# Stacked high and low keys and values, third units in the output bank, and the scaling of the probabilities on ScalarE

## The chip, the cores and the metric

The kernel runs on one core of a Trainium2 chip, in one launch. The metric is the device time of that launch in microseconds (us), lower is better. Engines: PE is TensorE (matmuls and transposes), ACT is ScalarE, DVE is VectorE, POOL is GpSimd, SP is the queue that issues the weight loads.

## The reference

One decoder layer over 512 tokens of width 1024 in float32: a SwiGLU, a mixer, a cross-attention to 256 memory tokens, a second SwiGLU, each with a norm before and after. The mixer runs two head groups on one input projection. The part that the change touches is the "fox" attention, 8 heads of width 64, and the scaling of the probabilities in the memory attention (4 heads of width 256):

```python
s = einsum('bhqd,bhkd->bhqk', q, k) * Dh ** -0.5
s = s + c[t] - c[s]            # c: running sum of log forget gates, per head
s = where(k_pos <= q_pos, s, -inf)
p = softmax(s, axis=-1)
o = einsum('bhqk,bhkd->bhqd', p, v)
```

## The kernel before

Every float32 product is made of three faster ones: each operand is split into a rounded high part and the rest (low), and the kernel adds high x high, low x high and high x low in the accumulator. The helper `three` (L1424) issues these three matmuls. The high part is written by ACT (a copy that rounds), the low part by DVE (a subtraction). The weights go the same way: SP loads a block of 1024 columns, ACT rounds it (L634, w_hi), POOL subtracts (L578, w_lo); PE waits for both.

The fox attention is cut into 32 units: unit k is head k // 4 and query block i = k % 4, with 128 (i + 1) keys. The four engines each run a loop over steps k, written out by hand. In step k,

- PE: scores of unit k (mask product L1719, then the three products; at least 256 keys wide), `fill(k)`: one or two quarters (six matmuls of 512 columns each) of the three input projections that are still left, spread over the steps by the table FILL; if unit k - 3 ends a head, the product of its four probability blocks with the values (`output`, 12 matmuls into bank 3); then the transposes of unit k - 2 (L1731, one per 128 keys, into bank 2).
- ACT: the exponential of unit k with its sum (L841), the rounding of a weight block if one is due (`round_to`, in the steps 4, 7, 9, 12, 15, 18, 20, 23, 27, 30 and 32), the high part of the transposed probabilities of unit k - 2 (L851), and for a head that has ended the high part of its output (L832). In each step with i = 3 it first spreads the next head's running sum (L821).
- DVE: the maximum of unit k (L1155), reciprocal and scaling of unit k - 1 (L1128, L1130, `normalise`), the low part of the transposed unit k - 2 (L1168), the low part of an ended head's output (L1142); around steps 10 to 14 also the evacuation of a finished projection and three multiplications by decays (L1297).

Every queue is served in order. PE's transposes of unit k - 2 wait for its scaled probabilities (normed) and for the low part of unit k - 3 (pt_l), because both units use bank 2. A head's output waits for pt_l of its last unit and for the low part of the output before (y_l), because all heads use bank 3.

FILL gives one quarter to steps 1, 4, 5, 8, 9, 11, 12, 13, 16, 17, 20, 21, 23, 24, 25, 27, 28, 29, 33 and 34, none to step 0, and two to the others. Of the steps with i = 3, therefore, 11, 23 and 27 have one quarter.

Ahead of the attention ACT and DVE evacuate the projections of q, k and v (`in_evacuate`): per group of 128 columns DVE scales into tmp (L1272), ACT rounds (L792 for q, L795 for k, L799 for v), DVE subtracts (L1280, L1284, L1288). PE's first fill waits for the low values of the first two token blocks. Behind the attention the gated linear attention (`gla`) starts with a warm-up product (L1435) once bank 3 is read out, and then waits for ACT's two copies L906. The memory attention runs the same kind of loop over 16 units, with the scaling by the same helper `normalise`.

Of the kernel before, what the change touches and what calls it, by code (L numbers as in the profile page):

```python
# [35 lines left out]
P = 128  # L36
# [139 lines left out]
def build(nc, a, out):  # L176
    ctx = ExitStack()
    with ctx:
# [73 lines left out]
        k_hi_a = sb("k_hi_a", [P, 2, SEQ], F32R, at=shared + 102 * kib)  # L252
        k_hi_b = sb("k_hi_b", [P, 2, SEQ], F32R, at=shared + 60 * kib)
        k_lo = sb("k_lo", [P, 4, SEQ], F32R, at=shared + 72 * kib)
        v_hi = sb("v_hi", [P, TC, FOX_W], F32R, at=shared + 32 * kib)
        v_lo = sb("v_lo", [P, TC, FOX_W], F32R, at=shared + 40 * kib)
# [21 lines left out]
        fox_hi, fox_lo = (t[:, :, :].rearrange("p (c e) n -> p c e n", e=2)[:, :, 0, :] for t in (q_hi, q_lo))  # L278

# [70 lines left out]
        q_zero = sem("q_zero")  # L350
        q_even_hi = sem("q_even_hi")
# [16 lines left out]
        y_l = sem("y_l")  # L368

# [68 lines left out]
        def key_hi(c):  # L438
            return (k_hi_a, k_hi_b)[c // 2][:, c % 2, :]
# [9 lines left out]
        def s_bank(k):  # L449
            return bank[fox_slot(k) % 2]  # L450

# [115 lines left out]
        def _(gp):  # L567
# [45 lines left out]
            for n, t in enumerate((q_hi, q_lo)):  # L613
                for e in range(2):
                    heads = t[FOX_D * (1 - e):FOX_D * (2 - e), :, :].rearrange("p (c e) n -> p c e n", e=2)
                    gp.memset(heads[:, :, e, :].bitcast(F32), 0.0).then_inc(q_zero, 1)  # L616
                    gp.wait_ge(q_zero, 2 * n + e + 1)
# [10 lines left out]
        def _(act):  # L628
# [156 lines left out]
            def in_evacuate(g, ms=range(4)):  # L785
                b = bank[IN_BANK[g]:IN_BANK[g] + 4]
                for m in ms:
# [5 lines left out]
                    elif g == 1:  # L793
                        act.wait_ge(in_tmp, 4 + m + 1)
                        act.activation(key_hi(m), tmp[:, m, :], ACT.Copy).then_inc(in_hi, 1)  # L795
                    elif g in (2, 4):
                        wait_group(act, g, m)
                        act.wait_ge(hinv, 2)
                        act.activation((v_hi if g == 2 else gv)[:, m, :], b[m][:, :], ACT.Copy,  # L799
                                       scale=rinv_tok[:, m:m + 1]).then_inc(in_hi, 1)  # L800
# [21 lines left out]

            def fox_attention():

                def output(done):
# [5 lines left out]
                    r = slice(FOX_D * (hd % 2), FOX_D * (hd % 2 + 1))  # L831
                    act.activation(fox_hi[r, hd // 2, :], bank[3][r, :], ACT.Copy).then_inc(y_h, 1)  # L832

                for k in range(N_FOX + LATE + 2):
                    if k < N_FOX - 1 and k % TC == TC - 1:
                        cum_spread(k // TC + 1)
                    if k < N_FOX:
# [4 lines left out]
                                       bias=nmx[:, r], scale=-1.0, accum_out=rs[:, r]).then_inc(expd, 1)  # L842
                    if k <= N_FOX + LATE:
                        round_to(B_IN + KB * FILL_GROUPS[0] + 2 + sum(FILL[:k]) // 4)
                    if 0 <= k - LATE < N_FOX:
# [3 lines left out]
                        if hd:  # L849
                            act.wait_ge(pv_done, hd)  # L850
                        act.activation(pt_hi[:, 0:nk, i * P:(i + 1) * P],  # L851
                                       bank[2][:, 0:nk * P].rearrange("p (j n) -> p j n", n=P),
                                       ACT.Copy).then_inc(pt_h, 1)
                    output(k - LATE - 1)
                    if k == PAIR_TURN[1]:
# [4 lines left out]
            def mem_attention():  # L860
# [10 lines left out]
                for k in range(len(MEM_UNITS) + LATE + 1):  # L871
                    u = N_FOX + k
                    if k < len(MEM_UNITS):
# [4 lines left out]
                                       scale=rinv_tok[:, i:i + 1], accum_out=rs[:, r]).then_inc(expd, 1)  # L878
                    output(k - LATE - 1)
# [61 lines left out]
            def mixer():  # L941
# [8 lines left out]
                round_to(B_IN + KB * 2 + 3)  # L950
                in_evacuate(1, (0, 1))
# [62 lines left out]
        def _(dve):  # L1014
# [109 lines left out]
            def normalise(u, w):  # L1124
# [4 lines left out]
                dve.wait_ge(rsum, u + 1)  # L1129
                dve.tensor_scalar(prob[:, u % PROBS, 0:w], prob[:, u % PROBS, 0:w], rr[:, r], None,  # L1130
                                  ALU.mult).then_inc(normed, 1)

            def fox_attention():

                def output(done):
# [4 lines left out]
                    r, c = slice(FOX_D * (hd % 2), FOX_D * (hd % 2 + 1)), hd // 2  # L1140
# [942 lines left out]
```

## Time and profile before

| | us |
| --- | --- |
| median of 3 runs | 1178.94 (1178.93 to 1179.42) |
| the profiled execution, its own time | 1180.76 |
| the profile's span | 1179.0 |
| PE busy | 1157.9 (98%) |
| ACT busy | 451.6 (38%) |
| DVE busy | 356.2 (30%) |
| POOL busy | 490.1 (42%) |

The profile is of one execution. Its span is the time between the first and the last instruction on record; 1.8 us of the execution's time lie outside it. The granted clock of TensorE was 0.999 over the span. A matmul's duration on record overlaps its successor's, so what a matmul takes of PE's time is the distance between two starts. DVE, ACT and POOL serve one instruction after the other, and their durations can be added, less about 0.1 us of overlap for each on ACT.

### The profile page before, as it was taken

Reading aid. Unit: us, or ns where it says so; the run is one execution under the profiler, and the core shown is the slowest. Engines: PE = TensorE matmul, PEld = TensorE weight load, DVE = VectorE, ACT = ScalarE, POOL = GpSimd, SP = SyncE. Lnnn points to the kernel's source line nnn. Section 1 sums busy time; section 2 is a strip of 40 time slices with the busy share of each in tenths; the row PEclk is TensorE's granted clock in tenths of the full one; section 3 lists DMA queues with packets and bytes.
Section 4 is the critical chain, followed back from the end, with each engine's and each line's share of the span. In section 5 each row is a group of like instructions: output and inputs, shape, how many; then the busy total and the mean of one; then the engine's idle time right before and its main releaser. Section 6 shows DMA issues by size and latency. Waiting matters only on the chain.

```text
span 1179.0 us, 15227 instructions
## 1 busy us (share of the span) xinstructions
PE 1157.9 (98%) x5664; PEld 964.8 (82%) x5664; DVE 356.2 (30%) x718; ACT 451.6 (38%) x740; POOL 490.1 (42%) x223
## 2 busy tenths in 40 slices
PE   8999999999999999999999999999999999999998
PEld 7888888888888878787778988878888888888886
DVE  2131221220005274655554204744131131130003
ACT  6232232231215456455625534545433232232113
POOL 5444344344442633222314863425435435434441
PEclk9999999999999999999999999999999999999999
DMA  6232332322222222111213442213333333222232
GB/s 201 90 106 91 93 103 89 107 89 99 98 90 89 72 90 87 41 55 52 90 54 108 161 160 91 80 54 119 103 93 93 103 89 107 89 98 99 90 107 108
DMA packets 84989, 113.03 MB, mean 96 GB/s; under 512 B 8846, under 2 KB 53964, under 8 KB 84940
## 3 DMA queue, kind: packets, MB, share of 16 engines
q1 hardware_dynamic: 84848, 112.34, 29.5%
q8 instruction: 33, 0.54, 0.2%
q14 instruction: 16, 0.13, 0.0%
q10 hardware_dynamic: 92, 0.02, 0.0%
HBM read 110.24 MB, written 2.10 MB: 95 GB/s over the span
## 4 chain that ended last, share of the span: by engine, by line
PE 62%; issue 24%; POOL 10%; DVE 2%; DMA 1%; ACT 0%; POOLq 0%; SPq 0%; DVEq 0%; ACTq 0%
PE bank L1426 14%; PE bank L1430 13%; PE bank L1427 13%; POOL w_lo L578 10%; PE bank L1566 7%; PE bank L1572 6%; PE bank L1567 6%; PE bank L1467 1%; DVE h L1063 1%; DMA raw<-in_ffn_w_gu 1%; POOL q_hi L616 0%; POOL q_lo L616 0%; PE bank L1503 0%; DVE tmp L1052 0%; DMA raw<-in_mix_w_in 0%
## 5 line engine op out<-in xcount | busy, mean ns | idle before, releaser
L578 POOL TENSOR_TENSOR w_lo<-raw,w_hi 128x1024 fp32r<-128x1024 f32 x200 | 478.9, 2404 | 666.4 <-ACT w_hi L634 665.9
L1426 PE MATMUL bank<-xh,w_hi 128*128 128x512 f32 (+1 forms) x912 | 349.6, 383 | 0.1
L1427 PE MATMUL bank<-xh,w_lo 128*128 128x512 f32 (+1 forms) x912 | 348.3, 382 | 0.0
L1430 PE MATMUL bank<-xl,w_hi 128*128 128x512 f32 (+1 forms) x912 | 348.3, 382 | 0.0
L634 ACT ACTIVATE w_hi<-raw 128x1024 fp32r<-128x1024 f32 x200 | 209.0, 1057 | 350.8 <-DMA raw<-in_ffn_w_down 167.5
L1430 PEld LDWEIGHTS bank<-xl,w_hi 128*128 128x128 f32 x912 | 171.4, 188 | 33.6
L1426 PEld LDWEIGHTS bank<-xh,w_hi 128*128 128x128 f32 x912 | 171.5, 188 | 33.1 <-issue 0.8
L1427 PEld LDWEIGHTS bank<-xh,w_lo 128*128 128x128 f32 x912 | 171.5, 188 | 32.0
L1566 PE MATMUL bank<-w_hi,mid_hi 128*128 128x512 f32 x352 | 137.2, 390 | 0.0
L1567 PE MATMUL bank<-w_hi,mid_lo 128*128 128x512 f32 x352 | 137.0, 389 | 0.0
L1097 DVE TENSOR_TENSOR tmp<-bank,rinv 128x512 f32<-128x512 f32 x44 | 30.2, 685 | 343.7 <-PE bank L1430 327.7
L1572 PE MATMUL bank<-w_lo,mid_hi 128*128 128x512 f32 x352 | 130.5, 389 | 0.0
L743 ACT ACTIVATE tmp<-tmp 128x512 f32<-128x512 f32 x44 | 27.9, 633 | 152.3 <-DVE tmp L1097 152.3
L1566 PEld LDWEIGHTS bank<-w_hi,mid_hi 128*128 128x128 f32 x352 | 66.1, 188 | 14.1 <-DVE tmp L1098 0.6
L1567 PEld LDWEIGHTS bank<-w_hi,mid_lo 128*128 128x128 f32 x352 | 66.1, 188 | 13.7
L1572 PEld LDWEIGHTS bank<-w_lo,mid_hi 128*128 128x128 f32 x352 | 66.1, 188 | 13.7
L1052 DVE SCALAR_TENSOR_TENSOR bank<-bank,g_row 128x512 f32<-128x512 f32 x20 | 13.8, 690 | 129.7 <-ACT sq L681 129.7
L1566 PE MATMUL bank<-w_hi,xh 128*128 128x512 f32 x96 | 38.6, 402 | 2.0 <-POOL w_lo L578 1.1
L1052 DVE SCALAR_TENSOR_TENSOR tmp<-bank,g_row 128x512 f32<-128x512 f32 x12 | 8.2, 682 | 105.8 <-ACT sq L681 105.8
L1567 PE MATMUL bank<-w_hi,xl 128*128 128x512 f32 x96 | 37.5, 391 | 0.0
L1572 PE MATMUL bank<-w_lo,xh 128*128 128x512 f32 x96 | 36.3, 392 | 1.1 <-POOL w_lo L578 1.1
L1130 DVE TENSOR_SCALAR prob<-prob,rr 128x256 f32<-128x256 f32 (+3 forms) x48 | 35.0, 729 | 1.7
(238 smaller groups left out, 1283.8 us busy)
## 6 DMA issues: line engine op xcount, KB each, us to landing
raw<-in_ffn_w_gu SPq DMA_DIRECT2D x176, 256.0 KB, 2.9
raw<-in_ffn_w_down SPq DMA_DIRECT2D x88, 256.0 KB, 2.8
raw<-in_mix_w_in SPq DMA_DIRECT2D x48, 256.0 KB, 2.8
raw<-in_mem_w_kv SPq DMA_DIRECT2D x32, 256.0 KB, 3.1
raw<-in_mem_w_o SPq DMA_DIRECT2D x24, 256.0 KB, 2.9
raw<-in_mix_w_out SPq DMA_DIRECT2D x16, 256.0 KB, 3.0
raw<-in_mem_w_q SPq DMA_DIRECT2D x16, 256.0 KB, 2.8
h<-in_x SPq DMA_DIRECT2D x4, 512.0 KB, 6.3
```

The lines of the kernel that those rows point to most:

```text
L578: gp.tensor_tensor(w_lo[:, n % SLOTS, :], raw[:, n % SLOTS, :], w_hi[:, n % SLOTS, :].bitcast(F32), ALU.subtract).then_inc(lo_ready, 1)
L634: act.activation(w_hi[:, n % SLOTS, :], raw[:, n % SLOTS, :], ACT.Copy).then_inc(hi_ready, 1)
L743: act.activation(tmp[:, pair, :], tmp[:, pair, :], ACT.Silu).then_inc(silu_done, 1)
L1052: dve.scalar_tensor_tensor(out=weighted_at(n)[:, :], in0=out_bank(s, n)[:, :], scalar=POST_SCALE[s], in1=g_row[:, cols], op0=ALU.mult, op1 ...
L1097: dve.tensor_tensor(tmp[:, pair, :], b[pair][:, :], rinv[:, :], ALU.mult).then_inc(gate_scaled, 1)
L1130: dve.tensor_scalar(prob[:, u % PROBS, 0:w], prob[:, u % PROBS, 0:w], rr[:, r], None, ALU.mult).then_inc(normed, 1)
L1426: pe.matmul(dst, w[0], x[0], start=start, stop=False, skip_group_check=loose)
L1427: pe.matmul(dst, w[1], x[0], start=False, stop=False, skip_group_check=loose)
L1430: return pe.matmul(dst, w[0], x[1], start=False, stop=stop, skip_group_check=loose)
L1566: pe.matmul(dst, x[0][:, tok], w[0][:, cols], start=start, stop=False, skip_group_check=True)
L1567: pe.matmul(dst, x[1][:, tok], w[0][:, cols], start=False, stop=False, skip_group_check=True)
L1572: return pe.matmul(out_bank(s, m)[:, :], x[0][:, tok], w[1][:, cols], start=False, stop=end, skip_group_check=True)
```

## The change

Keys: each fox head gets a tile of its own (`key_hl`) with its high part in 64 of the 128 rows and its low part in the other 64. Queries: the high part is written to both halves of the rows (8 further copies on ACT, `query_twins`), the low part keeps zeros in the other half. Scores are then two products instead of three. Values: each head's 64 high and 64 low columns lie side by side (`v_hl`), so the product with the probabilities gives high rows and low rows in one pass, two products instead of three for each of the four blocks. The two halves of bank 3 then have to be added: ACT copies one half out (`fox_y`, y_part), DVE adds the other (y_sum, bank 3 is free again), ACT rounds (y_h, `round_rows`) and DVE subtracts (y_l, `low_rows`) one step later.

In the diff the first `normalise` is ACT's, the second DVE's.

Units with i = 2 are transposed into bank 3, which then waits for y_sum of the output before; units with i = 3 wait for the low part of unit i = 1 instead of that of their predecessor. The scaling of the probabilities (`normalise`) moves from DVE to ACT in both attentions, in step k for unit k - 1, between the exponential and the rounding of a weight block; DVE keeps the reciprocal (`inverse_sum`). POOL clears half as many tiles ahead of the attention.

```diff
+            def query_twins():
+                for hd in range(FOX_H):
+                    act.activation(q_hi[head_rows(hd + 1), hd, :], tmp[head_rows(hd), hd // 2, :],
+                                   ACT.Copy).then_inc(q_twin, 1)
...
-                        act.activation(key_hi(m), tmp[:, m, :], ACT.Copy).then_inc(in_hi, 1)
+                        for e, done in enumerate((k_even_hi, in_hi)):
+                            r = head_rows(e)
+                            act.activation(key_hl(2 * m + e)[r, :], tmp[r, m, :], ACT.Copy).then_inc(done, 1)
...
+            def normalise(u, w):
+                r = slice(u % 4, u % 4 + 1)
+                act.wait_ge(rsum, u + 1)
+                act.activation(prob[:, u % PROBS, 0:w], prob[:, u % PROBS, 0:w], ACT.Copy,
+                               scale=rr[:, r]).then_inc(normed, 1)
...
-                    act.activation(fox_hi[r, hd // 2, :], bank[3][r, :], ACT.Copy).then_inc(y_h, 1)
+                    r, other = fox_rows_of(hd), fox_rows_of(hd + 1)
+                    act.activation(fox_y[r, hd // 2, :], bank[3][other, :], ACT.Copy).then_inc(y_part, 1)
+                def round_rows(done):
...
+                    act.wait_ge(y_sum, hd + 1)
+                    act.activation(fox_hi[r, hd // 2, :], fox_y[r, hd // 2, :], ACT.Copy).then_inc(y_h, 1)
...
+                    if 0 < k <= N_FOX:
+                        normalise(k - 1, key_width(FOX_UNITS[k - 1][1]))
                     if k <= N_FOX + LATE:
                         round_to(B_IN + KB * FILL_GROUPS[0] + 2 + sum(FILL[:k]) // 4)
...
                     output(k - LATE - 1)
+                    round_rows(k - LATE - 2)
...
-            def normalise(u, w):
+            def inverse_sum(u):
                 dve.wait_ge(expd, u + 1)
                 dve.reciprocal(rr[:, r], rs[:, r]).then_inc(rsum, 1)
-                dve.wait_ge(rsum, u + 1)
-                dve.tensor_scalar(prob[:, u % PROBS, 0:w], prob[:, u % PROBS, 0:w], rr[:, r], None,
-                                  ALU.mult).then_inc(normed, 1)
...
+                    dve.wait_ge(y_part, hd + 1)
+                    dve.tensor_tensor(fox_y[r, c, :], bank[3][r, :], fox_y[r, c, :],
+                                      ALU.add).then_inc(y_sum, 1)
+                def low_rows(done):
...
                     dve.wait_ge(y_h, hd + 1)
-                    dve.tensor_tensor(fox_lo[r, c, :], bank[3][r, :], fox_hi[r, c, :].bitcast(F32),
+                    dve.tensor_tensor(fox_lo[r, c, :], fox_y[r, c, :], fox_hi[r, c, :].bitcast(F32),
                                       ALU.subtract).then_inc(y_l, 1)
...
-                    three(dst, (q_hi[:, hd, tok], q_lo[:, hd, tok]), (key_hi(c)[:, 0:w], k_lo[:, c, 0:w]),
-                          False, True, True).then_inc(scored, 1)
+                    pe.matmul(dst, q_hi[:, hd, tok], key_hl(hd)[:, 0:w], start=False, stop=False, skip_group_check=True)
+                    pe.matmul(dst, q_lo[:, hd, tok], key_hl(hd)[:, 0:w], start=False, stop=True,
+                              skip_group_check=True).then_inc(scored, 1)
...
-                    if k:
-                        pe.wait_ge(pt_l, k)
+                    hd, i = FOX_UNITS[k]
+                    if i == TC - 2:
+                        if hd:
+                            pe.wait_ge(y_sum, hd)
+                    elif k:
+                        pe.wait_ge(pt_l, k - 1 if i == TC - 1 else k)
...
-                        last = three(bank[3][:, q0:SEQ],
-                                     (v_hi[:, j, c * P:(c + 1) * P], v_lo[:, j, c * P:(c + 1) * P]),
-                                     (pt_hi[:, j, q0:SEQ], pt_lo[:, j, q0:SEQ]), j == 0, j == TC - 1, True)
+                        for pt in (pt_hi, pt_lo):
+                            last = pe.matmul(bank[3][:, q0:SEQ], v_hl[:, j, hd, :], pt[:, j, q0:SEQ],
+                                             start=j == 0 and pt is pt_hi, stop=j == TC - 1 and pt is pt_lo,
+                                             skip_group_check=True)
```

## Rows read from the trace of the kernel before

**Rows 1.** The page, part 1: busy us (share of the span) x instructions of each engine.
```profile
PE 1157.9 (98%) x5664; PEld 964.8 (82%) x5664; DVE 356.2 (30%) x718; ACT 451.6 (38%) x740; POOL 490.1 (42%) x223
```

**Rows 2.** Busy time by engine over the fox attention: us, PE, PEld, DVE, ACT, POOL, clock, DMA.
```profile
452.50:570.50 118.00, 114.19 (x602) 95.19 (x601) 67.09 (x183) 55.21 (x128) 28.71 (x12) 1.00 0.18 57
```

**Rows 3.** PE in order of time, the score products: start us, us, instruction.
```profile
452.77 0.28 PE L1427 MATMUL bank<-k_hi_a,q_lo 128*128 128x256 f32 x1
452.89 0.28 PE L1430 MATMUL bank<-k_lo,q_hi 128*128 128x256 f32 x1
...
458.97 0.39 PE L1427 MATMUL bank<-k_hi_a,q_lo 128*128 128x512 f32 x1
459.20 0.39 PE L1430 MATMUL bank<-k_lo,q_hi 128*128 128x512 f32 x1
```

**Rows 4.** PE, idle before the transposes L1731 of the attention (us, times).
```profile
  DVE pt_lo L1168: 2.5, 4
```

**Rows 5.** The start of the stage, ACT, DVE and PE in order of time [idle before].
```profile
451.57 0.75 DVE L1288 SCALAR_TENSOR_TENSOR v_lo<-bank,rinv_tok,v_hi 128x512 fp32r<-128x512 f32 x1 [7.79 <-ACT v_hi L799]
...
453.49 0.40 PE L1426 MATMUL bank<-xh,w_hi 128*128 128x512 f32 x1
```

**Rows 6.** Forms by line from 400 to 570 us: x | busy us, mean ns | idle before.
```profile
L1142 DVE TENSOR_TENSOR q_lo<-bank,q_hi 64x512 fp32r<-64x512 f32 x7 | 4.8, 688 | 1.7 <-ACT q_hi L832 1.7
...
L792 ACT ACTIVATE q_hi<-tmp 64x512 fp32r<-64x512 f32 x8 | 5.0, 630 | 1.4 <-DVE tmp L1272 1.2
...
L851 ACT ACTIVATE pt_hi<-bank 128x512 fp32r<-128x512 f32 x8 | 4.7, 585 | 1.4 <-PE bank L1731 1.4
...
L795 ACT ACTIVATE k_hi_b<-tmp 128x512 fp32r<-128x512 f32 x2 | 1.2, 624 | 0.0
```

**Rows 7.** ACT and PE in head 5, from the one transpose at 530.71.
```profile
530.71 0.27 PE L1731 MATMUL bank<-ident,prob 128*128 128x128 f32 x1
...
538.41 0.41 PE L1731 MATMUL bank<-ident,prob 128*128 128x128 f32 x2
...
533.28 0.72 ACT L841 ACTIVATE prob<-prob,nmx 128x512 f32<-128x512 f32 x1
...
533.99 1.06 ACT L634 ACTIVATE w_hi<-raw 128x1024 fp32r<-128x1024 f32 x1
534.94 0.38 ACT L851 ACTIVATE pt_hi<-bank 128x256 fp32r<-128x256 f32 x1
536.01 0.40 ACT L841 ACTIVATE prob<-prob,nmx 128x128 f32<-128x128 f32 x1 [0.69 <-DVE nmx L1155]
```

**Rows 8.** POOL and DVE in order of time, where both read SBUF.
```profile
433.88 2.40 POOL L578 TENSOR_TENSOR w_lo<-raw,w_hi 128x1024 fp32r<-128x1024 f32 x1 [3.48 <-ACT w_hi L634]
...
535.13 2.39 POOL L578 TENSOR_TENSOR w_lo<-raw,w_hi 128x1024 fp32r<-128x1024 f32 x1 [9.05 <-ACT w_hi L634]
548.74 2.38 POOL L578 TENSOR_TENSOR w_lo<-raw,w_hi 128x1024 fp32r<-128x1024 f32 x1 [11.23 <-ACT w_hi L634]
...
433.95 2.88 DVE L1238 TENSOR_TENSOR ls_min<-ls_min,ls_abs 128x512 f32<-128x512 f32 x1
...
535.35 0.42 DVE L1168 TENSOR_TENSOR pt_lo<-bank,pt_hi 128x256 fp32r<-128x256 f32 x1 [1.73 <-ACT pt_hi L851]
...
536.09 1.71 DVE L1130 TENSOR_SCALAR prob<-prob,rr 128x512 f32<-128x512 f32 x1
```

**Rows 9.** DVE and PE in head 2, which carries the decays.
```profile
495.36 2.64 DVE L1297 TENSOR_TENSOR gq<-tmp,gq 128x1024 f32<-128x1024 f32 x1
...
500.24 0.50 PE L1426 MATMUL bank<-pt_hi,v_hi 128*128 128x512 f32 x1 [0.62 <-DVE pt_lo L1168]
```

**Rows 10.** The end of the stage, ACT and PE.
```profile
571.14 1.08 ACT L906 ACTIVATE gla_a<-bank 128x512 f32<-128x512 f32 x2
...
571.90 1.13 PE L1435 MATMUL bank<-ones 128*128 128x512 f32 x2 [0.54 <-DVE q_lo L1142]
```

**Rows 11.** The page, part 5: the scaling of both attentions on DVE.
```profile
L1130 DVE TENSOR_SCALAR prob<-prob,rr 128x256 f32<-128x256 f32 (+3 forms) x48 | 35.0, 729 | 1.7
```

More of the change, by code:

```diff
@@ L251, in build @@
         q_lo = sb("q_lo", [P, FOX_H, SEQ], F32R, at=shared + 16 * kib)
[L252 to L256, printed above, removed]
+        k_hl_a = sb("k_hl_a", [P, 2, SEQ], F32R, at=shared + 102 * kib)
+        k_hl_b = sb("k_hl_b", [P, 4, SEQ], F32R, at=shared + 72 * kib)
+        k_hl_c = sb("k_hl_c", [P, 2, SEQ], F32R, at=shared + 60 * kib)
+        v_hl = sb("v_hl", [P, TC, FOX_H, P], F32R, at=shared + 32 * kib)
+        v_hi, v_lo = v_hl[:, :, :, 0:FOX_D], v_hl[:, :, :, FOX_D:P]
         gq = sb("gq", [P, 2, SEQ], at=shared + 48 * kib)
@@ L350, in build @@
         q_zero = sem("q_zero")
+        q_twin = sem("q_twin")
+        k_even_hi = sem("k_even_hi")
+        k_even_lo = sem("k_even_lo")
         q_even_hi = sem("q_even_hi")
@@ L368, in build @@
         y_l = sem("y_l")
+        y_part = sem("y_part")
+        y_sum = sem("y_sum")
         ke_turned = sem("ke_turned")
@@ L450, in s_bank, with fp_bank @@
             return bank[fox_slot(k) % 2]
+        def fp_bank(k):
+            return bank[3 if k % TC == TC - 2 else 2]
         def key_width(i):
@@ L612, in _ @@
             gp.wait_ge(lo_ready, B_IN + 6)
[L613 to L617, printed above, removed]
+            for e in range(2):
+                heads = q_lo[head_rows(e + 1), :, :].rearrange("p (c e) n -> p c e n", e=2)
+                gp.memset(heads[:, :, e, :].bitcast(F32), 0.0).then_inc(q_zero, 1)
+                gp.wait_ge(q_zero, e + 1)
             for n in range(B_IN + 6, -(-(B_IN + 6) // SLOTS) * SLOTS):
@@ L798, in in_evacuate @@
                         act.wait_ge(hinv, 2)
-                        act.activation((v_hi if g == 2 else gv)[:, m, :], b[m][:, :], ACT.Copy,
-                                       scale=rinv_tok[:, m:m + 1]).then_inc(in_hi, 1)
+                        dst, src = gv[:, m, :], b[m][:, :]
+                        if g == 2:
+                            dst, src = v_hi[:, m, :, :], src.rearrange("p (h d) -> p h d", d=FOX_D)
+                        act.activation(dst, src, ACT.Copy, scale=rinv_tok[:, m:m + 1]).then_inc(in_hi, 1)
                     elif g == 5:
@@ L1172, in fox_attention @@
                     output(k - LATE - 1)
+                    low_rows(k - LATE - 2)
                     for g in (3, 5):
@@ L1715, in scores @@
                     dst, tok = s_bank(k)[:, 0:w], slice(i * P, (i + 1) * P)
-                    c, part = hd // 2, slice(0, 2) if i else slice(1, 3)
+                    part = slice(0, 2) if i else slice(1, 3)
                     if hd == FOX_H // 2 and i == 0:
+                        pe.wait_ge(k_even_lo, 4)
                         pe.wait_ge(in_lo, 12)
@@ L1741, in output @@
                     if hd:
-                        pe.wait_ge(y_l, hd)
+                        pe.wait_ge(y_sum, hd)
                     else:
@@ L1904, in gla @@
                     last.then_inc(ke_turned, 1)
-                pe.wait_ge(y_l, Y_FOX)
+                pe.wait_ge(y_sum, Y_FOX)
                 warm_up(bank[2], 1)
```

60 lines of the change are left out of this document (43 added, 17 removed).

## The prediction

> **What bounds the kernel now.** I read the page first: PE is busy for 98% of the span [rows 1], so the time is PE's own instructions plus the few places where PE waits. Then the windows: the fox attention lasts 118.0 us, PE is busy in 114.2 of them, DVE in 67, ACT in 55 [rows 2]. Only here and in the memory attention does the change touch work, and the granted clock is 1.00, so all prices are at the full clock. Third, PE in order of time: two score products of 256 columns start 0.12 us apart, two of 512 columns 0.23 [rows 3]; 384 columns lie between, 0.17. Fourth, PE's waits: the transposes wait for pt_lo, the low part that DVE writes, 2.5 us in 4 places [rows 4]. Last, ACT, DVE and POOL around one such wait, for their order [rows 7, 8]. The reader is to see that PE has the work, but that ACT and DVE hand units to it through two in-order queues with little to spare in the steps with one quarter of fill.
>
> **The change, part by part.** *Products.* Each head loses four score products (256, 256, 384, 512 columns) and four value products (512, 384, 256, 256): 2 x (0.23 + 0.17 + 0.12 + 0.12) = 1.28 us a head, 10.2 us for eight. This is certain, and it is the whole gain on PE. Everything else is about what ACT and DVE do when PE comes sooner.
>
> *Ahead of the attention.* The eight query twins cost 8 x 0.63 [rows 6] = 5.0 us on ACT, right where DVE has its idle 7.8 us before v_lo and ACT waits for DVE to reach the keys: hidden; uncovered they would cost at most 5. But each pair of key copies becomes four of half the rows, and 64 rows cost what 128 do (630 against 624 ns [rows 6]): +1.3 us for heads 0 to 3, +1.3 for heads 4 to 7, both ahead of v_hi on ACT; of the first, some 0.8 hides in an idle wait of ACT. v_lo then starts 1.8 us later than 451.57, its two instructions (0.75 each) end at 454.9, and PE's first fill, before at 453.49, starts at about 455.0 [rows 5]: +1.6 with the second wait behind it. POOL's smaller clearing frees POOL when nothing waits for it: 0.
>
> *Scaling on ACT.* No row shows it; the nearest are ACT's copies, 0.38 us for 256 columns [rows 7] and 0.585 for 512 [rows 6]; below, 0.1 less each by overlap; above, the exponential of 512 columns with 0.72 [rows 7]. I take the copies, because it is one. It sits behind the exponential and in front of the rounding and pt_hi, so pt_hi comes 0.2 to 0.5 later in every step. DVE loses 32 scalings here, 729 ns on average [rows 11], most of it from blocking (below).
>
> *Bank 3 for the third unit.* The waits of [rows 4] go: the third unit no longer waits for the second's low part, nor the fourth for the third's. y_sum takes the place of y_l with equal instructions, so heads hand over bank 3 as before.
>
> *The head's output.* ACT has one more copy per head (0.59) and DVE one more subtraction (0.69 unblocked, as L1142 [rows 6]), both in the step with i = 3, in front of the next maximum. low_rows is new in kind: both inputs lie in SBUF, where L1142 had one in PSUM. POOL and such an instruction exclude each other here: L1238 came 0.07 us behind a POOL subtraction and took 2.88 us instead of about 0.7, ending 0.55 after POOL; the scaling at 536.09 took 1.71; pt_lo at 535.35, which reads PSUM, took 0.42 within the same POOL instruction [rows 8]. The Trainium skill says so too (SBUF — State Buffer, section "SBUF: two separate sides": whichever starts first holds the shared port pair for its whole instruction, also against a DVE instruction with two SBUF inputs); by it low_rows waits out POOL, by DVE's bare rate it would take 0.69, and the traces agree with the first; the whole comes to 1181.6 by the first and to rival A's 1175.0 by the second.
>
> *One head, worked out.* Zero is 530.71 [rows 7]. The block rounded in step 23 starts at 533.99 = 3.3, behind the exponential; now the scaling of 384 columns is first: 3.7. POOL starts 1.14 behind the rounding (535.13 - 533.99) and lasts 2.4: 4.8 to 7.2. pt_hi starts 0.95 behind the rounding, 4.65; y_h follows, 4.9 to 5.5; low_rows is ready at 5.6, inside POOL's time, and ends at 7.2 + 0.55 = 7.75. Behind it on DVE are the maximum of unit 24 (0.3), then on ACT its exponential, at 8.0 (before: 536.01 = 5.3), 0.4, and the scaling of unit 23, 0.6: 9.0. For that PE waits with the transposes of unit 23, before at 538.41 = 7.7: +1.3. Behind them until the next head PE saves 0.17 + 0.64, so the head takes 0.5 longer than before.
>
> *The sum over the heads.* A block is rounded in the same step as low_rows in steps 7, 15, 23 and 27; step 27 is like 23 (POOL at 548.74 [rows 8]): +0.5 each. Step 7 has two quarters, PE comes 1.36 later: the wait is 0.9, and 0.7 more before the value product, because step 9 rounds too: -1.3 + 1.6 = +0.3, with rests +0.6. Head 2: its value product waits for pt_lo at 500.24 already [rows 9]; ahead of that on the chain now stand the scaling of units 10, 11, 12 (0.4, 0.5, 0.2) and y_h with low_rows (0.8): +1.9, less the 0.64 of the shorter product: +1.2. The decay at 495.36 took 2.64 behind POOL and does so again. Head 3: a decay (1.2) now behind y_sum delays the maximum by 0.9, then low_rows as above: +1.3. Head 4 has no such collision: -1.3. The last head: -1.28 + 0.35 of wait: -0.9. The first: +1.6 - 1.3 = +0.3. Behind the attention ACT must do y_h before its two copies (1.08 [rows 10]); they end 3.1 us behind the last product, the warm-up (1.13) 2.6: +0.5. Memory attention: 16 scalings of 0.38 on ACT in steps of over 3 us: 0; uncovered, 0.3 each. Sum: 0.3 + 0.6 + 1.2 + 1.3 - 1.3 + 0.5 + 0.5 - 0.9 + 0.5 = +2.7 us. The profiled execution (span 1179.0, own time 1180.8) would come to 1183.5; the median of the runs is 1.8 lower, 1178.9 + 2.7 = 1181.6.
>
> **The rivals.** *A: low_rows isn't held, or not in front of PE (faster).* If POOL has not started when it comes, or it is the later one, low_rows ends at 6.3 instead of 7.75; each of the heads with steps 23 and 27 then gains 1.4, step 15 1.9, step 7 1.9: 6.6 less, 1175.0. For it: PE's queue may have slack I took too small, and [rows 8] has few cases. Against: ACT's order fixes POOL's start 0.8 us ahead of low_rows. *B: the work removed is the gain (faster still).* The new waits stay within those removed: 1178.9 - 10.2 = 1168.7, with the 2.5 of [rows 4] 1166. For it: PE is 98% busy. Against: the idle 3.8 us of the stage already stem from these queues. *C: the lateness reaches the value products (slower).* pt_lo of a head's last unit leaves PE only 0.3 us in the heads with a collision, by the same chain; if every link (waits between engines, scaling as dear as the exponential) takes 0.1 more, PE waits again there, 0.7 in each of five heads: 1185.1. *D: the twins or key copies reach the weights.* ACT's rounding for the last block ahead of the attention comes 1.3 late, and POOL then has 0.3 to spare: at most 1 us, within the range.
>
> **How the numbers follow.** 0.2% (2.4 us) is about what a measurement of this kernel can tell from no change. Forecast 0.44 (1178.5 to 1184 for itself), A 0.28, B 0.07, C 0.21. Slower by over 2.4 us begins at 1181.3: half of the forecast and nearly all of C, 0.42. Faster ends at 1176.6: B, most of A, 0.32. The rest 0.26. The range takes in A with its lower side and C: 1172 to 1186; below lies B with some of A, above a tail of C.
>
> **What would show it.** In the profile after: PE with 64 matmuls fewer (5600); PE's idle time in the stage up from 3.8 to some 16 us; the transposes L1731's successor waiting for the scaling on ACT in heads 1, 3, 5 and 6 by 1 to 3 us; low_rows at over 2 us four times out of eight, 0.7 otherwise; the first fill at 455. Wrong if low_rows is short throughout, if the waits of PE move to pt_lo, or if head 2 is no longer than before.

## The result and the profile after

| | before | after |
| --- | --- | --- |
| median of 5 runs, us | 1178.94 (1178.92 to 1179.42) | 1188.56 (1187.15 to 1192.11) |
| ratio | | 1.0085, 95% interval 1.0075 to 1.0096 |
| profiled execution, own time / span, us | 1180.76 / 1179.0 | 1192.11 / 1190.4 |
| granted clock over the span | 0.999 | 0.992 |

The change makes the kernel 9.6 us slower. The point forecast had the direction right (slower by 2.7), the size not: 1181.6 had been predicted, with 1186 as the upper end. The profiled execution is the longest of the five; the others ran at a clock of 0.994 to 0.996, and the shortest, 1187.15 us, had the highest. So the time after goes with the clock; in the kernel before it was 0.998 or more in all executions beside the experiments below.

The page of the changed kernel, part 1:

```profile
PE 1157.1 (97%) x5600; PEld 961.7 (81%) x5600; DVE 338.5 (28%) x682; ACT 484.2 (41%) x808; POOL 485.7 (41%) x221
```

PE has the 64 matmuls fewer that were foreseen, and yet 0.8 us less busy time only, against 10.2 expected [rows 1]. The windows of the changed kernel say why (us, then PE, PEld, DVE, ACT and POOL busy, the granted clock, DMA). The first is the whole fox attention, the others are parts of it:

```profile
452.10:581.00 128.90, 112.13 (x536) 91.34 (x535) 61.43 (x161) 75.59 (x170) 28.71 (x12) 0.93 0.16 50
480.00:500.00 20.00, 16.46 (x76) 12.89 (x76) 10.06 (x28) 11.04 (x25) 4.43 (x2) 0.91 0.14 45
500.00:520.00 20.00, 15.53 (x71) 12.44 (x70) 11.58 (x26) 9.76 (x24) 2.72 (x2) 0.91 0.17 52
520.00:540.00 20.00, 19.40 (x101) 16.07 (x100) 7.63 (x26) 15.29 (x34) 4.82 (x2) 1.00 0.17 54
540.00:560.00 20.00, 16.42 (x79) 13.23 (x77) 8.96 (x20) 10.80 (x24) 4.76 (x2) 0.91 0.09 29
560.00:575.00 15.00, 13.09 (x53) 11.06 (x54) 5.61 (x19) 8.01 (x19) 2.40 (x1) 0.77 0.14 45
```

Two things are new beside [rows 2]. PE is idle for 16.8 of 128.9 us instead of 3.8 of 118.0, as forecast ("up to some 16"). And the clock, which was 1.00 in the whole stage, is 0.93: this was in no step of the prediction. PE in order of time around the transposes of unit 23, in head 5, shows both:

```profile
545.83 0.66 PE L1801 MATMUL bank<-ident,prob 128*128 128x128 f32 x4 [2.47 <-ACT prob L855]
...
547.03 0.44 PE L1491 MATMUL bank<-xh,w_lo 128*128 128x512 f32 x1
547.26 0.63 PE L1494 MATMUL bank<-xl,w_hi 128*128 128x512 f32 x1
547.69 0.63 PE L1490 MATMUL bank<-xh,w_hi 128*128 128x512 f32 x1
548.12 0.63 PE L1491 MATMUL bank<-xh,w_lo 128*128 128x512 f32 x1
...
550.67 0.40 PE L1491 MATMUL bank<-xh,w_lo 128*128 128x512 f32 x1
550.90 0.40 PE L1494 MATMUL bank<-xl,w_hi 128*128 128x512 f32 x1
```

Products of 512 columns start 0.23 us apart up to 547.26 and again from 550.67, and 0.43 apart between: PE is at the lower of its two levels (1.2 instead of 2.4 GHz) for some 3.4 us, from 1.4 us after it has waited for the scaled probabilities. The same follows the waits that end at 516.6 (products 0.43 apart up to 519.6) and at 561.9 (from 563.7 to 567.5); there the four transposes right behind the wait are at the lower level already (1.11 us for the four, 0.66 in head 5). The waits of PE in the stage of the changed kernel (us in total, times, longest):

```profile
PE bank L1801 <- ACT prob L855: 9.0, 5, 3.0
PE bank L1490 <- DVE tmp L1332: 2.5, 2, 2.1
PE bank L1818 <- DVE pt_lo L1225: 2.1, 3, 1.3
PE bank L1490 <- DVE v_hl L1351: 1.8, 1, 1.8
PE bank L1490 <- POOL w_lo L597: 0.9, 1, 0.9
```

In the kernel before, PE waited in this stage for pt_lo, 2.5 us ahead of the transposes [rows 4] and 0.62 ahead of one value product [rows 9], and hardly for anything else. L1801 are the transposes, L855 is the scaling on ACT, L1818 are the value products. Now the chain ahead of unit 23, lines of ACT, POOL and DVE of the changed kernel in order of time, with some left out between; the one transpose that was taken as zero is at 536.28 here:

```profile
536.28 0.27 PE L1801 MATMUL bank<-ident,prob 128*128 128x128 f32 x1
...
539.15 0.73 ACT L885 ACTIVATE prob<-prob,nmx 128x512 f32<-128x512 f32 x1
539.85 0.62 ACT L855 ACTIVATE prob<-prob,rr 128x384 f32<-128x384 f32 x1
540.36 1.06 ACT L652 ACTIVATE w_hi<-raw 128x1024 fp32r<-128x1024 f32 x1
541.31 0.39 ACT L897 ACTIVATE pt_hi<-bank 128x256 fp32r<-128x256 f32 x1
541.50 2.39 POOL L597 TENSOR_TENSOR w_lo<-raw,w_hi 128x1024 fp32r<-128x1024 f32 x1 [7.62 <-ACT w_hi L652]
541.57 0.63 ACT L876 ACTIVATE q_hi<-q_flat 64x512 fp32r<-64x512 f32 x1
542.23 2.20 DVE L1199 TENSOR_TENSOR q_lo<-q_flat,q_hi 64x512 fp32r<-64x512 f32 x1
544.36 0.27 DVE L1212 CUSTOM_DVE_ANT_0 prob<-bank,cum_b 128x128 f32<-128x128 f32 x1
544.67 0.40 ACT L885 ACTIVATE prob<-prob,nmx 128x128 f32<-128x128 f32 x1 [2.48 <-DVE nmx L1212]
545.07 0.71 ACT L855 ACTIVATE prob<-prob,rr 128x512 f32<-128x512 f32 x1
```

L1199 is low_rows, L876 round_rows, L597 GpSimd's subtraction. Read from the bottom: PE waits for the scaling of unit 23, which is behind the exponential of unit 24, which waits 2.48 us for the maximum of unit 24, which is behind low_rows, and low_rows takes 2.20 us and ends 0.5 after POOL's subtraction. It has the links of the forecast, in their order; how long they are comes below.

### The profile page after: what moved, and what is told of

It is laid out like the page before. It is cut to its first block, busy times and chain, and to the rows that moved or that the text cites. A ratio compares the mean times of both kernels' runs of the same rounds, so it can differ in the third digit from the quotient of the medians.

```text
span 1190.4 us, 15133 instructions
## 1 busy us (share of the span) xinstructions
PE 1157.1 (97%) x5600; PEld 961.7 (81%) x5600; DVE 338.5 (28%) x682; ACT 484.2 (41%) x808; POOL 485.7 (41%) x221
## 4 chain that ended last, share of the span: by engine, by line
PE 61%; issue 26%; POOL 10%; DVE 2%; DMA 1%; ACT 0%; POOLq 0%; SPq 0%; DVEq 0%; ACTq 0%
PE bank L1490 13%; PE bank L1491 13%; PE bank L1494 13%; POOL w_lo L597 10%; PE bank L1630 6%; PE bank L1631 6%; PE bank L1636 6%; PE bank L1531 1%; DVE h L1113 1%; DMA raw<-in_ffn_w_gu 1%; POOL q_lo L634 0%; PE bank L1567 0%; DVE tmp L1102 0%; DMA raw<-in_mix_w_in 0%; DVE bank L1102 0%
## 5 line engine op out<-in xcount | busy, mean ns | idle before, releaser
L597 POOL TENSOR_TENSOR w_lo<-raw,w_hi 128x1024 fp32r<-128x1024 f32 x200 | 478.2, 2401 | 682.3 <-ACT w_hi L652 681.9
L1636 PEld LDWEIGHTS bank<-w_lo,mid_hi 128*128 128x128 f32 x352 | 66.1, 188 | 13.8
L1102 DVE SCALAR_TENSOR_TENSOR bank<-bank,g_row 128x512 f32<-128x512 f32 x20 | 13.8, 692 | 129.4 <-ACT sq L699 129.4
L885 ACT ACTIVATE prob<-prob,nmx 128x128 f32<-128x128 f32 (+3 forms) x32 | 18.0, 563 | 41.3 <-DVE nmx L1212 41.3
```

The costliest lines, as they stand in the source:

```text
L597: gp.tensor_tensor(w_lo[:, n % SLOTS, :], raw[:, n % SLOTS, :], w_hi[:, n % SLOTS, :].bitcast(F32), ALU.subtract).then_inc(lo_ready, 1)
L885: act.activation(prob[:, k % PROBS, 0:w], prob[:, k % PROBS, 0:w], ACT.Exp, bias=nmx[:, r], scale=-1.0, accum_out=rs[:, r]).then_inc(expd, 1)
L1102: dve.scalar_tensor_tensor(out=weighted_at(n)[:, :], in0=out_bank(s, n)[:, :], scalar=POST_SCALE[s], in1=g_row[:, cols], op0=ALU.mult, op1 ...
L1636: return pe.matmul(out_bank(s, m)[:, :], x[0][:, tok], w[1][:, cols], start=False, stop=end, skip_group_check=True)
```

## The experiments

Each was timed beside the kernel before, on the same chip; 5 to 8 on another chip than the rest. The kernel before ran at 1179.16 us beside 1 to 4, 1179.29 beside 5 to 8 and 1179.04 beside 9 to 12. Where medians of different groups are subtracted below, this 0.25 us is the least that they are uncertain by. The changed kernel was not timed again: whatever is subtracted from its 1188.56 us also carries its scatter, 1187.15 to 1192.11. Experiments 1 to 8 and 10 to 12 start from the changed kernel, 9 from the kernel before.

| # | kernel | us | ratio to before (95%) |
| --- | --- | --- | --- |
| 1 | scaling on DVE | 1180.14 | 1.0009 (0.9999 to 1.0019) |
| 2 | rows split three steps later | 1181.3 | 1.0019 (1.0009 to 1.0028) |
| 3 | both | 1174.72 | 0.9962 (0.9948 to 0.9976) |
| 4 | long waits of the transposes filled | 1185.77 | 1.0058 (1.0041 to 1.0075) |
| 5 | saved products put back | 1195.09 | 1.0135 (1.0118 to 1.0152) |
| 6 | third unit in bank 2 | 1195.14 | 1.0129 (1.0112 to 1.0146) |
| 7 | scaling on DVE, memory attention only | 1188.72 | 1.0082 (1.0065 to 1.0099) |
| 8 | 3 with the first values earlier | 1176.14 | 0.9967 (0.9957 to 0.9977) |
| 9 | before, with the fox scaling on ACT | 1183.22 | 1.0033 (1.0020 to 1.0045) |
| 10 | 3 with the saved products put back | 1181.91 | 1.0025 (1.0016 to 1.0035) |
| 11 | 3 with four scalings on ACT | 1173.46 | 0.9951 (0.9934 to 0.9967) |
| 12 | 4 with a fifth wait filled | 1186.18 | 1.0058 (1.0041 to 1.0075) |

**1. Scaling on DVE again, in both attentions.** ACT's two calls of `normalise` go, DVE's `inverse_sum` scales as well (only its new lines are shown):

```diff
 dve.reciprocal(rr[:, r], rs[:, r]).then_inc(rsum, 1)
+if scaled_width:
+    dve.wait_ge(rsum, u + 1)
+    dve.tensor_scalar(prob[:, u % PROBS, 0:scaled_width], prob[:, u % PROBS, 0:scaled_width], rr[:, r],
+                      None, ALU.mult).then_inc(normed, 1)
```

> The scaling of the probabilities goes back to DVE in both attentions; the stacked products, the units in bank 3 and the new path of the head's output stay. Theory L (low_rows, blocked behind POOL in steps 7, 15, 23 and 27, makes the long waits of PE; the scaling only lengthens ACT's queue by about 0.4 us a step): low_rows still lasts about 2.1 us four times, the waits before the transposes of units 15, 23 and 27 fall from 3.4, 2.9 and 3.4 us to about 2, and with them the stretches at the clock's lower level: 1179 to 1183. Theory S (the scaling on ACT, 0.70 us for 512 columns where a copy takes 0.585, is itself the loss): the waits shrink below 1 us, and the time falls below 1175.

1180.14 us (1178.07 to 1181.88), inside theory L's range: 8.4 of the 9.6 us are gone. low_rows is as long as in the change, four times over 2 us (first row, duration in ns: shortest, median, longest), and the transposes still wait, but three times and at most 2.0 us (second row). The profiled execution is the fastest of the ten, with a clock of 0.999; the ten fall apart by the clock: three at 1178.1 us with 0.999, seven at 1180.1 to 1181.9 with 0.995 or 0.996. So in this kernel too the clock is lowered more often than not, and those executions are 2 us or more longer. low_rows by its line, and one of the waits:

```profile
L1199 DVE TENSOR_TENSOR q_lo<-q_flat,q_hi x8: 685/1378/2209, 476.0 to 569.8; 64x512 fp32r<-64x512 f32 x8
```

```profile
PE bank L1801 <- DVE prob L1177: 5.4, 3, 2.0
```

**2. The rows split later.** ACT's round_rows and DVE's low_rows move from the step with i = 3 to the next one with i = 2, ahead of pt_hi and pt_lo there; the scaling stays on ACT. The same edit in both queues:

```diff
+if k <= N_FOX + LATE:
+    low_rows(k - LATE - TC - 1)
 if 0 <= k - LATE < N_FOX:
     ...
 output(k - LATE - 1)
-low_rows(k - LATE - 2)
+if k == N_FOX + LATE + 1:
+    low_rows(k - LATE - 2)
```

> Scaling on ACT as in the change, but the rounding and subtraction of a head's output (round_rows, low_rows) are moved by three steps, into the long step with i = 2 ahead of the transposed probabilities, where both engines wait for PE anyway. Theory L: low_rows no longer stands in front of the maximum of the next head's first unit, the waits of PE before units 15, 23 and 27 fall to under 1.2 us, the clock stays at its upper level, 1173 to 1178. Theory S: the waits stay over 2 us, above 1184.

1181.3 us, 7.3 us less than the change, but between the two theories and in neither range. The waits of the transposes for the scaling fell as theory L had it, to 1.0 at most and 3.4 us in all instead of 9.0; the time did not, since PE now waits for pt_lo. In their new place the rows are held by POOL twice of eight times (2.46 and 2.34 us, else 0.69), and pt_lo is late for it by 0.5 and 0.8 us (third row: L1807 are the transposes, L1824 the value products). The longest wait, 2.9 in head 2, has no row in front of it: it is behind a decay (L1367) that took 2.68 us, and kernel 4 below has the same one. DVE of this kernel in order of time, and its waits:

```profile
518.91 2.46 DVE L1202 TENSOR_TENSOR q_lo<-q_flat,q_hi 64x512 fp32r<-64x512 f32 x1 [2.57 <-ACT q_hi L876]
521.30 0.27 DVE L1230 TENSOR_TENSOR pt_lo<-bank,pt_hi 128x128 fp32r<-128x128 f32 x1
```

```profile
PE bank L1824 <- DVE pt_lo L1230: 4.6, 3, 2.9
PE bank L1807 <- ACT prob L855: 3.4, 6, 1.0
PE bank L1807 <- DVE pt_lo L1230: 1.4, 2, 0.8
```

**3. Both edits.**

> Both edits of the two runs before this one together: scaling on DVE, and the head's output rounded three steps later. If L and S are separate links of one chain, this is the fastest of the three, 1169 to 1173, with some 4 us of idle PE in the stage. If either alone is the loss, it equals the better of the two within 1 us.

1174.72 us (1174.14 to 1174.87), faster than both kernels and the fastest of the three, though 1.7 us above the range. The two edits bring 8.4 and 7.3 us by themselves and 13.8 together, so they are two links and not one; some 1.9 us of what each brings is the same.

**4. The long waits filled.** The changed kernel with 1, 10, 8 and 10 idle products of 512 columns ahead of the transposes of units 7, 15, 23 and 27, into the bank that these then overwrite:

```diff
-pe.wait_ge(normed, k + 1)
 hd, i = FOX_UNITS[k]
 ...
+for _ in range({7: 1, 15: 10, 23: 8, 27: 10}.get(k, 0)):
+    pe.matmul(fp_bank(k)[:, :], ident_r[:, :], xh[:, 0, :], start=True, stop=True, skip_group_check=True)
+pe.wait_ge(normed, k + 1)
```

> The change itself, and in PE's queue ahead of the wait for the scaled probabilities 1, 10, 8 and 10 products of 512 columns into bank 2 (units 7, 15, 23 and 27), whose results the transposes then overwrite: they fill waits and add no result. Theory C (a wait of 2.4 us or more is followed by some microseconds at 1.2 GHz, which cost time by themselves): matmuls after those three waits start 0.23 us apart instead of 0.43, and the time falls by 3 to 5 us, to 1184 or 1185. If the clock costs nothing because PE would wait again anyway: 1188 to 1189.

1185.77 us (1185.59 to 1186.16; the shortest of the change is 1187.15), theory C at a little less than its price: PE does 6.6 us more of useless work, and the kernel is 2.8 us faster. The windows over heads 5 and 6 have a clock of 1.00 where the change had 0.91 and 0.77:

```profile
540.00:560.00 20.00, 18.65 (x96) 15.33 (x95) 10.17 (x26) 10.83 (x27) 3.93 (x2) 1.00 0.16 53
560.00:575.00 15.00, 14.50 (x75) 11.88 (x74) 6.42 (x16) 8.30 (x17) 4.81 (x2) 1.00 0.16 52
```

**5. The saved products put back.** A third score product and a third value product, as repeats of products that are there; the output differs from the reference for it.

```diff
+pe.matmul(dst, q_lo[:, hd, tok], key_hl(hd)[:, 0:w], start=False, stop=False, skip_group_check=True)
 pe.matmul(dst, q_lo[:, hd, tok], key_hl(hd)[:, 0:w], start=False, stop=True,
           skip_group_check=True).then_inc(scored, 1)
...
-for pt in (pt_hi, pt_lo):
+for n, pt in enumerate((pt_hi, pt_lo, pt_lo)):
```

> The changed kernel with TensorE's saved work put back: a third product into every score unit and a third value product for every token block, 1.28 us a head or 10.2 us in all at the full clock; the repeated products stand in for the removed ones and change the output. Theory 1, the chain of ScalarE, VectorE and GpSimd sets the pace at the waits: much of the added work only fills waits, the clock stays at 1.00 for longer, and the time rises by 2 to 6 us, to 1190 to 1194. Theory 2, TensorE's work sets the pace: the whole 10 us is added, 1198.

1195.09 us, 6.5 more, just above the range of theory 1. Of the 10.2 us of products some 6.5 show even in a kernel that waits this much. The reading is that the steps behind a wait are PE's own and only what lies ahead of one is free; which products were free was not traced.

**6. The third unit back in bank 2**, with the old wait for the low part of the unit before:

```diff
-return bank[3 if k % TC == TC - 2 else 2]
+return bank[2]
...
-if i == TC - 2:
-    if hd:
-        pe.wait_ge(y_sum, hd)
-elif k:
-    pe.wait_ge(pt_l, k - 1 if i == TC - 1 else k)
+if k:
+    pe.wait_ge(pt_l, k)
```

> The changed kernel with the third unit of every head back in bank 2, as before, waiting for the low halves of the unit before; all else as changed. Theory 1, the place of the third unit only moves a score product and its wait by a few tenths of a microsecond, and what releases the turns is further down the chain: 1188 to 1190. Theory 2, the early third unit crowds ScalarE and VectorE in the last steps of a head and is part of the loss: 1184 to 1186. Theory 3, the early start is what the change has in its favour, and without it each head waits longer: 1192 or more.

1195.14 us, 6.6 more: theory 3. In its waits the low parts are back, and longer than [rows 4] had them, since pt_hi is later:

```profile
PE bank L1798 <- DVE pt_lo L1225: 17.4, 11, 2.5
```

**7. Scaling on DVE in the memory attention alone.**

```diff
-if 0 < k <= len(MEM_UNITS):
-    normalise(u - 1, NMEM)
...
-inverse_sum(u - 1)
+inverse_sum(u - 1, NMEM)
```

> The changed kernel with the probabilities of the memory attention alone scaled by VectorE again, as before; those of the forgetting attention stay on ScalarE. Theory 1, the memory attention keeps TensorE busy either way, so that the whole loss lies in the forgetting attention: 1188, within 0.7 us. Theory 2, a part of the 8.4 us that came back with both scalings on VectorE lay here: 1184 to 1186.

1188.72 us (1187.45 to 1190.69), nothing that can be told from the change: theory 1. From 740 to 800 us PE is busy for 56.50 us here and 56.81 in the change.

**8. Kernel 3 with the values of two token blocks ahead of the second pair of key copies on ACT** (DVE's waits for these copies are numbered anew):

```diff
-in_evacuate(1, (2, 3))
 in_evacuate(2, (0, 1))
+in_evacuate(1, (2, 3))
```

> Scaling on VectorE in both attentions and the split of the output rows three steps later, as in the version that ran at 1174.72, and besides it the high values of the first two token blocks ahead of the second pair of key copies on ScalarE. Theory 1, the first fill's wait of 2.04 us at 451.85 goes, since it waits for the low values, and with it the time falls by 1 to 2 us: 1173 to 1174. Theory 2, the key copies that are now later are wanted just as soon, and the wait moves there: 1174.7 or a little more.

1176.14 (1174.20 to 1176.38) against 1174.72 (1174.14 to 1174.87): no gain. The wait only moves, as theory 2 had it, though to the other values and not to the keys. The first fill starts at 451.85 without waiting; the second waits 2.00 us for the other two token blocks, whose v_lo starts at 454.31, since ACT has the key copies and a weight block ahead of them. PE and DVE of this kernel in order of time:

```profile
451.85 0.40 PE L1496 MATMUL bank<-xh,w_hi 128*128 128x512 f32 x1
...
454.31 1.41 DVE L1357 SCALAR_TENSOR_TENSOR v_hl<-bank,rinv_tok,v_hl 128x512 fp32r<-128x512 f32 x2 [2.32 <-ACT v_hl L822]
...
455.87 0.47 PE L1496 MATMUL bank<-xh,w_hi 128*128 128x512 f32 x1 [2.00 <-DVE v_hl L1357]
```

**9. The kernel before with one part of the change alone**: ACT scales the fox probabilities, behind the exponential of the next unit.

```diff
+if 0 < k <= N_FOX:
+    r, w = slice((k - 1) % 4, (k - 1) % 4 + 1), key_width(FOX_UNITS[k - 1][1])
+    act.wait_ge(rsum, k)
+    act.activation(prob[:, (k - 1) % PROBS, 0:w], prob[:, (k - 1) % PROBS, 0:w], ACT.Copy,
+                   scale=rr[:, r]).then_inc(normed, 1)
```

> The kernel before with one part of the change alone: ScalarE scales the probabilities of the forgetting attention, right after the exponential of the next unit. Products, banks, values and output rows are as before, and no row is split from SBUF. Theory 1, the scaling on ScalarE is dear wherever TensorE waits for it (0.38 to 0.70 us a unit, and behind the next exponential): 1183 to 1188. Theory 2, it is dear only together with the longer way of the output rows that the stacked values bring; alone it even goes past the scalings that GpSimd's subtraction holds on VectorE: 1178 to 1180.

1183.22 us, 4.2 more. It is dear by itself (theory 1), at the lower end. Ahead of the transposes PE waits for pt_lo 7 times instead of 4 [rows 4], for more than twice the time:

```profile
PE bank L1737 <- DVE pt_lo L1174: 5.9, 7, 1.6
```

**10. Kernel 3 with the saved products put back**, by the edit of experiment 5; the output differs.

> The version that ran at 1174.72 (scaling on VectorE, output rows split three steps later) with TensorE's saved products put back as repeats, 1.28 us a head or 10.2 us at the full clock; the output differs for it. Theory 1, some waits of 1 to 2.5 us are left in this version and take up a part of the work, as the changed kernel took up 3.7 of 10.2 us: 1179 to 1182. Theory 2, with the long waits gone TensorE's work is the bound and all of it shows: 1184 to 1185.

1181.91 us, 7.2 more than kernel 3. This is at the upper end of theory 1 and well below theory 2: the saved work is worth 7.2 of 10.2 us even here.

**11. Kernel 3 with the scaling of units 7, 15, 23 and 27 on ACT**, with a semaphore of its own.

```diff
+if k - 1 in ON_ACT:
+    normalise(k - 1, key_width(FOX_UNITS[k - 1][1]))
...
-inverse_sum(k - 1, key_width(FOX_UNITS[k - 1][1]))
+inverse_sum(k - 1, 0 if k - 1 in ON_ACT else key_width(FOX_UNITS[k - 1][1]))
...
-pe.wait_ge(normed, k + 1)
+if k in ON_ACT:
+    pe.wait_ge(normed_act, ON_ACT.index(k) + 1)
+else:
+    pe.wait_ge(normed, k + 1 - sum(n < k for n in ON_ACT))
```

> The version that ran at 1174.72, but with ScalarE scaling the four units 7, 15, 23 and 27, whose scaling on VectorE took 1.69 to 1.72 us beside GpSimd's subtraction. Theory 1, each of the four turns that wait for it is released 0.6 us sooner and VectorE is free 1.7 us sooner: 1172.5 to 1174. Theory 2, TensorE is released by something else there, or ScalarE has no room: 1174.7 or more.

1173.46 us (1173.37 to 1173.56), the fastest of all, 0.49% below the kernel before. Kernel 3 had this row among its waits, and this kernel has none of the kind:

```profile
PE bank L1807 <- DVE prob L1180: 2.8, 3, 1.7
```

The intervals of the two ratios overlap and the two were not timed together, so it is likely, not shown, that it beats kernel 3.

**12. A fifth wait filled**: kernel 4 with 12 idle products more, ahead of the value products of head 2.

```diff
+if hd == 2:
+    pe.wait_ge(pt_l, done)
+    pe.wait_ge(y_sum, hd)
+    for _ in range(12):
+        pe.matmul(bank[3][:, :], ident_r[:, :], xh[:, 0, :], start=True, stop=True, skip_group_check=True)
 pe.wait_ge(pt_l, done + 1)
```

> The changed kernel with idle products in five waits: those of the run that gave 1185.77, and 12 more ahead of the value products of the third head, where 3.34 us of waiting were left and the granted clock was 0.91 behind it. The products write a bank that is overwritten. Theory 1, the lowered clock costs time of its own: the clock is 1.00 in the whole stage and the time falls to 1183.5 to 1185. Theory 2, TensorE has slack behind that wait, and the clock there costs nothing: 1185.8.

1186.18 us: theory 2. The clock is 1.00 in every window now, that from 500 to 520 too (0.91 in kernel 4), and the time is the same within the runs. What PE gained there it waited for ahead of unit 15 (0.7 us behind the idle products, none in kernel 4).

## Why the prediction was wrong

By the starts of the one transpose (unit 4h), in us, the length of each head, and what was forecast for it. In kernel 4 the clock is mostly out of it, in kernel 1 the scaling on ACT. Each column is one execution, of the change the slowest of five and of kernel 1 the fastest of ten, so that the difference between these two is more than that of their medians:

| | before | after | difference | forecast | kernel 4 | kernel 1 |
| --- | --- | --- | --- | --- | --- | --- |
| head 0 | 13.91 | 12.61 | -1.30 | -1.3 | 12.63 | 12.60 |
| head 1 | 13.98 | 15.02 | +1.04 | +0.6 | 15.01 | 13.63 |
| head 2 | 16.12 | 17.94 | +1.82 | +1.2 | 18.79 | 16.55 |
| head 3 | 14.47 | 17.77 | +3.30 | +1.3 | 15.64 | 14.77 |
| head 4 | 13.95 | 13.15 | -0.80 | -1.3 | 13.38 | 12.61 |
| head 5 | 13.49 | 16.15 | +2.66 | +0.5 | 14.52 | 13.48 |
| head 6 | 13.60 | 17.18 | +3.58 | +0.5 | 14.52 | 13.46 |

The first transpose is 1.5 us later than before (forecast 1.6, which the row for head 0 leaves out), the first fill at 454.83 (forecast 455.0); the last stretch, up to the warm-up, is 1.0 shorter (forecast 0.9), and the copies behind it cost 0.7 (forecast 0.5). The sum over the heads is +10.3 in the profiled execution; 1.5 had been forecast.

**The step that failed** is the first one, "the granted clock is 1.00, so all prices are at the full clock". It was true of the trace of before and was taken over to a kernel for which the same text forecast waits of 1 to 3 us. Head 5 is the cleanest: its fourth transposes start 9.55 us after zero, 1.85 later than before; the work saved behind them is 0.81; without the clock the head would be 1.04 longer, and kernel 4, with the wait of the same length but filled, is 1.03 longer (14.52). The change is 2.66 longer; the other 1.63 are eight products at 0.43 instead of 0.23 apart. In head 6 the clock takes 17.18 - 14.52 = 2.66 in the same way. That is the profiled execution, the one with the lowest clock; by the medians the filled waits give back 2.8 us. The median is 7.0 us above the forecast, so this step accounts for 2.8 of them, and the greater part, 4.2, is the next term.

**A term that was mis-sized:** the waits themselves. With the clock taken out, kernel 4 still stands 6.6 us above before, where 2.7 had been forecast. That PE is idle for 16.8 us, as the forecast had it, is luck in part: the lowered clock stretched products into time that PE would have waited. In kernel 12, at 1.00 throughout, the same stage (452.10 to 574.57) has 9.8 us idle and 41 idle products at 0.23, 19.2 us together. One part of the term is the price of the scaling on ACT. Its row for 128 to 512 columns reads 0.39, 0.49, 0.60 and 0.71 us, against 0.28, 0.37, 0.47 and 0.58 of the copies that it was priced by; the bound from the exponential, 0.72, was nearly right, and the value should have been taken from that side. The forms of the changed kernel, 400 to 585 us:

```profile
L885 ACT ACTIVATE prob<-prob,nmx 128x512 f32<-128x512 f32 x8 | 5.8, 725 | 8.6 <-DVE nmx L1212 8.6
L855 ACT ACTIVATE prob<-prob,rr 128x512 f32<-128x512 f32 x8 | 5.7, 709 | 0.8 <-DVE rr L1178 0.8
...
L855 ACT ACTIVATE prob<-prob,rr 128x384 f32<-128x384 f32 x8 | 4.8, 604 | 0.0
...
L897 ACT ACTIVATE pt_hi<-bank 128x512 fp32r<-128x512 f32 x8 | 4.6, 578 | 1.1 <-PE bank L1801 1.1
...
L855 ACT ACTIVATE prob<-prob,rr 128x256 f32<-128x256 f32 x8 | 3.9, 494 | 0.0
```

In head 5 two such scalings are ahead of the transposes, 0.25 of the 0.55 us by which the chain was longer than worked out (9.0 forecast, 9.55 found); 0.3 is the exponential of unit 23, 2.87 after zero instead of 2.57. More came from places where the forecast charged nothing. In head 1 the fill of step 8 waits 0.9 us for w_lo of a block that ACT rounds behind the scaling, and the transposes of unit 7 only 0.2, where 1 to 3 had been forecast. Head 2 is the largest: in kernel 4 it is 2.67 longer than before, where 1.2 had been forecast. Besides the value product it waits 2.1 us for tmp (L1332, above), a finished projection that DVE evacuates in the same step behind low_rows; the kernel before waits 0.2 for it, and no term had it. Kernel 1 waits as long there, kernels 2 and 3, with the rows elsewhere, 1.1. Head 4 saved 0.80 instead of 1.3, and with the scaling on DVE it saves 1.34. The waits of L1818 (2.1 us, 3 times) are in heads 1, 2 and 4: the lateness reaches the value products, but not in heads 3, 5 and 6, where rival C had put most of it. Experiment 9 has the price alone, 4.2 us in a kernel with neither stacking nor rows to split, 0.3 to 0.6 in every head but head 2, which takes 1.4.

**What was right.** The products: 5600 matmuls; experiments 5 and 10 price them at 6.5 and 7.2 us; the other 3 to 4 of the 10.2 are taken to lie ahead of a wait. low_rows: eight of them, four at 2.17, 2.17, 2.20 and 2.05 us and the others at about 0.69, in the steps that were named. The Trainium skill (SBUF — State Buffer, section "SBUF: two separate sides") has the same exclusion, and these eight durations agree with it; rival A, which went by DVE's bare rate, falls with them. That the rows (round_rows and low_rows, moved together) stand on the path is shown by moving them: 7.3 us (experiment 2). The early third unit was costed as the end of the waits of [rows 4]; in the change it is worth 6.6 us (experiment 6), more than it removed, since without it the later pt_hi would have delayed pt_lo in 11 places. The memory attention was nothing (experiment 7). No wait for weights shows ahead of the attention, where rival D had put one. Rival B, the work removed as the gain, holds in part once both stalls are gone: kernels 3 and 11 are 4.4 and 5.6 us faster than the kernel before.

**Where the gain of 10.2 us went**, in the change: some 3.7 us of it never showed, presumably being ahead of waits; the other 6.5 and the 6.6 of bank 3 were paid for by three things, whose prices overlap and can't be added: the scaling on ACT (8.4 us, the clock's part in it), the split rows in their place behind POOL (5.4 us with the scaling on DVE, 7.3 with it on ACT), and the lowered clock (2.8 us). With one of the two stalls undone the longest wait of the transposes falls from 3.0 to 2.0 or 1.0 us. The clock recovers with it, but not wholly: from 0.992 to 0.996 in the five executions of the change to 0.995 to 0.999 in kernel 1, 0.997 to 1.000 in kernel 2 and 0.997 to 0.999 in kernel 3.

**Open.** Kernel 3 is left with, among shorter ones, one wait of 2.1 us for the value products of head 2, where the decays run on DVE, and one of 1.8 for the values' low parts at the start; the one version that was aimed at the second only moved it. How much of kernel 4's distance to the forecast belongs to each of its terms was not measured. Nor was it tried whether the weight blocks of steps 7, 15, 23 and 27 can be rounded in other steps.

## What to carry to other kernels

Work taken off an engine that is 98% busy need not pay in full; here 6.5 to 7.2 of 10.2 us showed. Price the chain through the other engines in the same detail as the work saved, and if it forecasts waits of 2 to 3 us on TensorE, price the products behind them at both levels of the clock. A subtraction with both inputs in SBUF on VectorE took 0.69 us alone and 2.05 to 2.47 beside GpSimd's, ending about 0.5 after it: look at what GpSimd does in that step before it is put in front of something that another engine waits for, and if it need not be done there, do it later.

## What the runs showed of the hardware

- The granted clock fell in a stage in which PE was 87% busy, after single waits of 2.5 to 3.0 us for the scaled probabilities, and came back after some 3 to 4 us of products. A wait by itself did not decide it: ahead of the fill at 495.74 PE waited 2.15 us in the change, and the products behind it started 0.43 apart, whereas kernel 1 waited 2.1 us for the same data with a clock of 1.00 in the windows around it. In kernel 8 a wait of 2.00 us in the first head was enough: the products from 456.44 on start 0.43 apart. Nor did the kernel decide it: of ten executions of kernel 1 three had a mean clock of 0.999 and took 1178.1 us, seven had 0.995 or 0.996 and took 1180.1 to 1181.9. What makes the difference was not found out.
- Idle products in front of a wait kept the clock at 1.00 behind it in heads 5 and 6, and 29 of them made the kernel 2.8 us faster.
- The subtraction of 64 x 512 with both inputs in SBUF took 2.05 to 2.20 us in the change where GpSimd's subtraction had started ahead of it, and 0.69 where not; pt_lo, which reads PSUM, took 0.43 us beside the same GpSimd instruction (541.73 us).
- A copy with a per-row scale from SBUF to SBUF on ACT takes 0.39 to 0.71 us for 128 to 512 columns, 0.11 to 0.13 more than the rounding copy out of the bank; as long as the exponential to within 0.02 us.
